# The row of the running maximum reaches all partitions by two GpSimd transfers instead of eight TensorE products

## The reference

```
b = jnp.cumsum(lf, axis=-1)
d = jnp.where(causal, b[..., :, None] - b[..., None, :] + li[..., None, :], -jnp.inf)
inter = b + m_prev[..., None]
m_t = jnp.maximum(inter, jnp.max(d, -1))
qk = jnp.einsum('bhtd,bhsd->bhts', q, k) * jnp.exp(d - m_t[..., None])
```

## Time and profile before

| | us |
|---|---|
| median of 3 runs | 930.28 |
| lowest, highest | 930.1, 931.82 |
| the profiled execution, its own time | 936.08 |
| its span, first to last instruction | 934.8 |
| TensorE busy | 894.8 (96%) |
| VectorE busy | 587.0 (63%) |
| ScalarE busy | 393.3 (42%) |
| GpSimd busy | 89.5 (10%) |

### The profile page before, as it was taken

How to read it: one execution, slowest core, us unless ns; L and a number is a source line. 1 busy time by engine, 2 the same in 40 slices (tenths; PEclk the granted TensorE clock), 3 DMA queues, 4 the chain that set the end, 5 groups by cost and what they waited for, 6 DMA issues and landing times.

```text
span 934.8 us, 14590 instructions
## 1 busy us (share of the span) xinstructions
PE 894.8 (96%) x6021; PEld 794.6 (85%) x6021; DVE 587.0 (63%) x825; ACT 393.3 (42%) x412; POOL 89.5 (10%) x86
## 2 busy tenths in 40 slices
PE   6999999999999999999999999989999999999974
PEld 6998889888899999999999997777888788888841
DVE  4633563645657272233233456789999999999945
ACT  4522131131332332322223104666777777777612
POOL 3000000000000001000101011301101011110034
PEclk9988999999999999999999997999999999999988
DMA  9763155284735042222322915799999999999548
GB/s 302 239 248 91 47 173 188 63 247 147 245 117 171 32 150 91 83 76 68 94 88 94 385 46 210 131 410 424 406 386 404 377 411 400 410 424 378 226 152 181
DMA packets 82932, 205.97 MB, mean 220 GB/s; under 512 B 5210, under 2 KB 58154, under 8 KB 70073
## 3 DMA queue, kind: packets, MB, share of 16 engines
q1 hardware_dynamic: 75080, 177.30, 52.8%
q0 software_dynamic: 7792, 27.81, 8.8%
HBM read 173.56 MB, written 33.75 MB: 222 GB/s over the span
## 4 chain that ended last, share of the span: by engine, by line
PE 73%; DVE 14%; issue 5%; DMA 4%; ACT 3%; POOL 1%; SPq 0%; DVEq 0%; ACTq 0%; POOLq 0%
PE psum L450 21%; PE psum L452 20%; PE psum L451 20%; DVE split_lo L1447 6%; DVE last_lo L1447 2%; PE psum L1888 2%; DMA raw<-in_w_e_up_dram 2%; PE psum L1898 2%; PE psum L2111 2%; PE psum L1927 1%; PE psum L2077 1%; DMA xn<-in_x_prompt_dram 1%; PE psum L1913 1%; DVE xgl L1607 1%; DMA ya_rows<-y_slots,dest_i 1%
## 5 line engine op out<-in xcount | busy, mean ns | idle before, releaser
L450 PE MATMUL psum<-x_hi,split_lo 128*128 128x272 f32 x704 | 209.9, 298 | 2.0 <-DVE pbl L1410 1.2
L452 PE MATMUL psum<-x_hi,split_hi 128*128 128x272 f32 x704 | 203.2, 289 | 0.0
L451 PE MATMUL psum<-x_lo,split_hi 128*128 128x272 f32 x704 | 203.0, 288 | 0.0
L1447 DVE TENSOR_TENSOR split_lo<-raw,split_hi 128x2048 fp32r<-128x2048 f32 x72 | 163.1, 2285 | 10.4 <-ACT split_hi L985 9.1
L985 ACT CAST split_hi<-raw 128x2048 fp32r<-128x2048 f32 x72 | 137.6, 1912 | 46.6 <-PE psum L452 40.2
L445 DVE TENSOR_TENSOR split_lo<-raw,split_hi 128x2048 fp32r<-128x2048 f32 x35 | 80.0, 2289 | 116.3 <-ACT split_hi L426 116.3
L450 PEld LDWEIGHTS psum<-x_hi,split_lo 128*128 128x128 f32 x704 | 133.6, 190 | 7.3 <-issue 2.7
L451 PEld LDWEIGHTS psum<-x_lo,split_hi 128*128 128x128 f32 x704 | 133.7, 190 | 1.4 <-issue 1.0
L452 PEld LDWEIGHTS psum<-x_hi,split_hi 128*128 128x128 f32 x704 | 133.5, 190 | 0.0
L450 PE MATMUL psum<-split_hi,xgl 128*128 128x512 f32 x188 | 75.3, 401 | 1.0 <-DVE xgl L1607 0.9
L451 PE MATMUL psum<-split_lo,xgh 128*128 128x512 f32 x188 | 73.7, 392 | 0.0
(11 more groups left out here) (378 smaller groups left out, 1780.2 us busy)
## 6 DMA issues: line engine op xcount, KB each, us to landing
raw<-in_w_e_gate_dram SPq DMA_DIRECT2D x32, 1024.0 KB, 8.5
raw<-in_w_e_up_dram SPq DMA_DIRECT2D x32, 1024.0 KB, 8.8
raw<-in_w_e_down_dram SPq DMA_DIRECT2D x32, 1024.0 KB, 7.9
raw<-in_w_in_dram SPq DMA_DIRECT2D x26, 1024.0 KB, 6.2
cb<-in_state_C_dram SPq DMA_DIRECT2D x8, 1024.0 KB, 8.2
out_dram<-cb SPq DMA_DIRECT2D x8, 1024.0 KB, 5.8
y_slots<-ys POOLq DMA_DIRECT2D x15, 512.0 KB, 8.6
kv<-kv_rows SPq DMA_DIRECT2D x4, 1028.0 KB, 8.0
```

The source lines that it names most:

```text
L450: nc.tensor.matmul(out, a_lo, b_hi, start=first, stop=False)
L451: nc.tensor.matmul(out, a_hi, b_lo, start=False, stop=False)
L452: return nc.tensor.matmul(out, a_hi, b_hi, start=False, stop=last)
L1447: v.tensor_tensor(lo, raw2[:, n % MOE_SLOTS, :], hi.bitcast(F32), ALU.subtract).then_inc(w_lo, 1)
```

## The change

A GpSimd store writes `nm` (4x544, 8.5 KB) to a scratch tensor in DRAM as soon as VectorE has made it. GpSimd then waits for that store and issues one load that reads the 2176 numbers 128 times and writes them to `bm`, all four heads at once (1088 KB in SBUF). The eight products of TensorE and the four copies of ScalarE are gone, and so are the four B units in the alternation of the PSUM banks (four, so later units keep the banks that they had). VectorE's `decay_start(h)`, which waited for ScalarE's copy of its own head, waits for the load instead. GpSimd's three stores to `y_slots` come behind both transfers in its stream.

```diff
@@ _wide_order
-    order += head(0) + [("B", h) for h in range(H)]
+    order += head(0)
@@ build
+    nm_rows = nc.dram_tensor("nm_rows", [H, N], F32).ap()
...
+    nm_ok, nm_out, bm_in = (sem(n) for n in ("nm_ok", "nm_out", "bm_in"))
@@ gpsimd
         pl.wait_ge(cst_in, 16)
+        pl.wait_ge(nm_ok, 1)
+        pl.dma_start(nm_rows, nm[:]).then_inc(nm_out, 16)
+        pl.wait_ge(nm_out, 16)
+        pl.dma_start(bm[:].rearrange("p h n -> p (h n)"), nm_rows.rearrange("h n -> (h n)").partition_broadcast(P)
+                     ).then_inc(bm_in, 16)
         pl.wait_ge(ready, H)
@@ scalar
         repeat_values(0)
-        for h in range(H):
-            j = Z["B", h]
-            ac.wait_ge(z_done, j + 1)
-            nc.scalar.copy(two(bm[:, h, :]), halves(j)).then_inc(z_free[j % 2], 1)
         dense_split_hi(ac, 5)
@@ vector
-        v.tensor_scalar(nm[:], m_r[:], -1.0, None, ALU.mult)
+        v.tensor_scalar(nm[:], m_r[:], -1.0, None, ALU.mult).then_inc(nm_ok, 1)
...
         def decay_start(h):
             c = ch[h % 2]
-            z_evacuated(ve_, Z["B", h])
+            ve_.wait_ge(bm_in, 16)
@@ tensor
         value_part(0, 0, 1)
-        for h in range(H):
-            j = Z["B", h]
-            z_room(pe, j)
-            for a in range(2):
-                last = mm(halves(j)[:, a, :], head_sel[:, whole(h)], nm[:, a * HALF:(a + 1) * HALF], start=True,
-                          stop=True)
-            last.then_inc(z_done, 1)
```

## The result

The changed kernel took 925.98 us (median of ten runs, 924.53 to 928.36) against 931.87 us of the kernel before (ten runs, 930.1 to 935.1). The ratio of the runs is 0.9928 (0.9914 to 0.9943), which is a gain of 6.7 us (5.3 to 8.0); the two medians differ by 5.9. The forecast was 921.1 us, a gain of 9.2, with a range up to 925.0. The sign and the mechanism held; the size did not, and the time lies 1 us outside the range of 918.3 to 925.0.

The account below looks back on a forecast made before the run. TensorE, busy 96% of the span, was taken as the bound. The terms -6.40 - 2.91 + 0.1 gave -9.2 us, so 930.28 became 921.1 us, with an 8-in-10 range of 918.3 to 925.0.

Parts of the forecast that it names:

- What bounds the kernel: TensorE, busy 96% of the span; the stretch from 64.35 to 80.56, 16.21 us, is entirely its own.
- First, the products' own time, 6.40 us: TensorE from 64.35 to 70.75: removing the products saves 6.40 us, including a 0.3 us wait and half-clock time.
- Second, the half clock that outlives them, 2.91: TensorE's key transposes to third transposes: 9.81 us in head 0 against 6.90 in head 1, so 2.91 saved.
- The base: Median of the runs shown, 930.28 us, 5.8 below the profiled 936.08; the gain of 9.2 was subtracted from it.
- inner band: Whole kernel: 919.3 to 923.0 us, from gain bounds of 8.5 to 9.4 and run scatter; chance 0.73.
- What is late next: VectorE's `kw` products before TensorE's third transposes: only just in time, 0.1 us lost, bounds 0 and 0.7.
- The transfers: GpSimd's store (3.1 us) and load (10 us) land at about 49, before VectorE's need at 62.83; no cost.
- The third rival's hold: GpSimd's store held behind VectorE's splits until 40.06, load landing at 69.7; gain 6.2, 924 to 927 us; chance 0.04.
- The break-even: Load landing at 75.9, past which TensorE's third transposes would start after 80.56 and the kernel be slower.
- that rival: Load lands past 75.9, 41 us after `nm` is ready, kernel slower; landing at 80 gives 934; chance 0.03.
- the clock did not fall for the transposes in place of the products: Rival at TensorE's key transposes: clock falls all the same, gain 6.3, 924.0 us; chance 0.12.
- given back in the expert stage: Rival: gain ends in the 16.95 us expert-chunk wait at 598; 925 to 930.3 us, part or whole; chance 0.08.

Follow-up runs that it names:

- the five profiles: The kernel before, unchanged, profiled five times: the prediction's execution at 936.08 us, then 936.36, 930.51, 932.17 and 929.08 us.
- the late version: Changed kernel with both transfers issued behind GpSimd's three stores to `y_slots`: 936.18 us, ratio to the kernel before 1.0041.

## Why the prediction was wrong

**What bounds the kernel:** right in place, and right for the execution that was read: forecast 9.2 us for the stretch, found 16.21 - 7.07 = 9.1 between the two profiles.

**The failed step is the two terms of TensorE.** "First, the products' own time, 6.40 us" and "Second, the half clock that outlives them, 2.91" were taken as what every execution pays. In the prediction's own terms, the five profiles give 6.40, 6.36, 4.63, 4.52 and 4.51 us for the first, 5.3 in the mean, and 2.91, 1.58, 1.58, 1.68 and 1.71 for the second, 1.9 in the mean. The clock's part in both together is 4.7 us in the profile that was read, and 1.6 in three of the four further ones. Split anew, an ordinary run has 4.5 us (products and wait at full clock) and some 2.5 us (the fall). The warning stood in the page: the profiled execution was 5.8 us longer than the median, and I subtracted the difference without asking which part of the span was longer.

**The base:** 930.28 us was the median of three runs; ten gave 931.87 and three further sets 932.3 to 933.4. That alone hid 1.6 us or more. From 931.87 the forecast would have been 922.7, and with the 7.0 us of the profiles it is 924.9, 1.1 us from the time found; that rest is within the interval of the gain, 5.3 to 8.0. The forecast's inner band has a slip that changes nothing: its own terms give 919.4 to 923.3, not 919.3 to 923.0.

**What is late next:** right. VectorE's second `kw` pair is just in time, and the profile shows no wait of TensorE for it; the third transposes came at 71.52, 71.25 forecast.

**The transfers:** right, and priced by the late version: not on the path, 4.8 us from landing to TensorE, paid in full past the slack. The third rival's hold, a store that waits until 40.06, did not come: the store was issued at 35.77 and had landed at 39.1. The break-even I gave, a landing at 75.9, was too generous: at 75.2 the kernel was already 3.8 us slower than before, because the gap brings its own fall (which I had named as possible) and because the ordinary kernel before is not the long execution. The argument against that rival was also too strong: to land 41 us after `nm` is ready, the load would have to take some 37 us, which is twice the broadcast row's time per byte (8.6 us for 512 KB), not four times.

**Rivals:** the clock did not fall for the transposes in place of the products, in any of three profiles. The Trainium skill ("TensorE: Matmul & The Clock Gate", Part 4) says that a transpose does not count as activity for the clock the way a matmul does. That made no difference here: eight transposes at the place, 0.87 us of work, left the clock at 1.00 each time. Nothing was given back in the expert stage. The rival that happened, a shorter fall in the kernel before, was not in the list; "by one or two microseconds either way" was there only for falls later in the program.

## What to carry to other kernels

A clock fall in one profile is a sample: before it is put into a sum, read how the profiled time stands to the timed runs, and take the fall's cost from its shortest form to its longest. Products over few partitions (here 4 of 128) can cost more than their own time where TensorE is busy before and behind them; widening the operands with zeros removed that part by itself. A small transfer that goes through DRAM is free only as long as its place in the queue leaves it the slack, so issue it ahead of the large ones, not behind.

## What the runs showed of the hardware

A product whose operands have 4 partitions of 128 runs about as long as a full one (3.86 against 3.67 us for sixteen instructions). During or behind eight such products TensorE's clock fell from 2.4 to 1.2 GHz in all six profiles that have them, for 3.4, 6.8 or 10.2 us by the execution; behind the same products over 128 partitions, zeros in all but four, it did not (one profile, and the granted clock of the timed runs). Behind the 15 transposes and 4 small products at 46 us it fell in nine of twelve profiles. Reading one 8.5 KB row of DRAM 128 times into 128 partitions took 8.3 us where the DMA engines were 97% busy (39.4 to 47.7 us) and 5.9 us where they were 56% busy (in the late kernel), 1088 KB in all; the median of the plain 1 MB chunks is 6.2 us.
